# First-half products moved ahead of two phase boundaries, a compact third span of attention, and an earlier fetch of held outputs

## The chip, the cores and the metric

The kernel runs on one core of a Trainium2 chip. The metric is device time in microseconds (us). TensorE (PE in the rows; its weight loads PEld) multiplies, VectorE (DVE), ScalarE (ACT) and GpSimd (POOL) work elementwise, SyncE (SP) issues the DMAs. SBUF is the working memory, PSUM (8 banks of 128 x 512 fp32) takes what TensorE writes.

## The reference

One step of a two-layer decoder trunk over 512 prompt tokens and 8 x 4 sample tokens, 544 in all, with a model width of 1024. Layer 0 is attention, layer 1 a Mamba-2 (SSD) mixer.

```python
for i in range(DEPTH):
    up, us = rmsnorm(hp, norm_pre[i]), rmsnorm(hs, norm_pre[i])
    if i % N_MIXERS == 0:
        yp, bufs_p = attn_prompt(up, attn_w_in[j], attn_w_out[j])
        ...
    else:
        yp, hp_new, cp_new = ssd_mixer(up, ssd_w_in[j], ...)
        ...
    hp = hp + rmsnorm(yp, norm_post[i])
    hs = hs + rmsnorm(ys, norm_post[i])
```

Attention has three spans, each with its own 16 query heads, 4 key heads and 4 value heads of 128:

```python
DILATED_GROUPS = ((128, 1), (512, 4), (2048, 16))
for g, (win, dil) in enumerate(DILATED_GROUPS):
    o, lse = banded_attention(to_strided(qs[g], dil), to_strided(ks[g], dil),
                              to_strided(vs[g], dil), win // dil)
y = merge_groups(outs, lses).reshape(n, l, ATTN_WIDTH).astype(u.dtype)
return (y * jax.nn.silu(gate)) @ w_out, bufs
```

In the third span the 512 prompt tokens fall into 16 residue classes of 32 tokens. A query reads only keys of its own class, so of a block of 128 queries by 128 keys (4 classes) only the four 32 x 32 squares on the diagonal are real; the rest is masked.

## The kernel before

**Phases.** `norm_phase` n0 (L138), `attention_phase` (L622), `mix_phase` m1 (L285), `ssd_phase` (L1549 on), `mix_phase` m2. Each is a block of its own with one instruction stream per engine. Between two blocks all engines meet at a barrier: no instruction of the next block, a DMA's issue included, starts before every engine has ended the last one (in the rows these waits carry lines L2527 to L2543).

**Projections.** The activations are kept feature by feature as `uhi` and `ulo` (high and low part, 8 x 128 features by 544 tokens). A weight tile is 1024 x 128. It is loaded to `w`, ACT copies its high part to `whi`, POOL (attention) or DVE (elsewhere) makes `wlo`, and PE does for each of 8 k blocks three products (whi by uhi, whi by ulo, wlo by uhi) on two halves of 272 tokens: 48 matmuls of 128 x 272 a tile. `w`, `whi`, `wlo` and the output banks have two slots; tile t uses slot t % 2, and may start when its `wlo` is there and the output of tile t-2 has been taken (`proj_free`). Each phase has these output banks as its own (`proj`, in the mix phase `acc`).

**Small items.** Between the quarters of a projection tile PE runs items of a hand-written table (ATTN_AHEAD for the group whose tiles are being made, ATTN_BEHIND for the group before it; SCAN and SETUP with slot times in the SSD phase, where a tile has four slots). Four head groups go through 22 tiles each. Items here: S (scores of a head in a span, L928), SC and SN (scores of the samples, L943), PT (transpose of the scaled probabilities of a unit to `small`, L902, then an ACT copy to `probs_t`, L1060), and, one PT later, `weigh` (L1002), which multiplies them by the values.

**Norm phase n0.** For five blocks of rows: square sum (ACT), inverse and `normed` (DVE, L254), transposes (PE, L191), high (ACT) and low part (DVE, L259). It also splits the first two weight tiles (`w_low` L263).

**Attention, start.** SP issues weight tiles 2 and 3, then the tables cos, sin, masks, mask_s, order and member (L817 to L822). DVE's first instruction waits for all six:

```python
dve.wait_ge(consts_in, 96)
```

Tile 0 is a key tile: DVE rotates it (L1187 to L1190) and then frees its output slot, which tile 2 needs.

**Attention, end.** The last stage does 8 output tiles. Near its end ACT and DVE split the operands of the rest of that product over `uhi` and `ulo` (L1105, L1329), k block by k block as PE's last tile gives them free; four of the eight come back from DRAM first (L834, the held outputs), issued by SP in its step t == 6.

**Mix phase.** PE ends the product, turns rows back, then DVE and ACT norm rows, add the residual (L508), and, in m1, do the pre-norm of layer 1 with PE transposes (L390), `uhi` (L440) and `ulo` (L529) as in n0. The transposes use the banks of `acc`.

**SSD, start.** SP issues the rows of PAR, then the dt weights and three vectors (`wd_in`, L1735), weight tiles 2 and 3, six tables. ACT's first work waits for the dt vectors (L2107). On PE the item PAR stands in slot 1, DT 0 in slot 4 and DT 1 in slot 7.

## Time and profile before

| | us |
|---|---|
| median of three runs | 1431.95 (1427.76 to 1433.5) |
| the profiled execution, its own time | 1431.52 |
| its span in the trace | 1429.7 |
| PE busy / PEld busy | 1336.1 (93%) / 1284.0 (90%) |
| DVE busy / ACT busy / POOL busy | 781.6 / 641.8 / 467.8 |

Stages of the span: n0 up to 24.8, attention to 821.7, m1 to 903.3, SSD to 1363.2, m2 to the end. PE has gaps only around the four boundaries and in parts of the SSD phase. A matmul in the trace may be one record or two: one on plain fp32 data (S, SC, SN, `weigh`) leaves two, one of the projections or a transpose leaves one.

### The profile page before, as it was taken

Reading aid. Unit: us, or ns where it says so; the run is one execution under the profiler, and the core shown is the slowest. Engines: PE = TensorE matmul, PEld = TensorE weight load, DVE = VectorE, ACT = ScalarE, POOL = GpSimd, SP = SyncE. Lnnn points to the kernel's source line nnn. Section 1 sums busy time; section 2 is a strip of 40 time slices with the busy share of each in tenths; the row PEclk is TensorE's granted clock in tenths of the full one; section 3 lists DMA queues with packets and bytes.
Section 4 is the critical chain, followed back from the end, with each engine's and each line's share of the span. In section 5 each row is a group of like instructions: output and inputs, shape, how many; then the busy total and the mean of one; then the engine's idle time right before and its main releaser. Section 6 shows DMA issues by size and latency. Waiting matters only on the chain. (4 is left out here: it accounts for less than half of the span.)

```text
span 1429.7 us, 29707 instructions
## 1 busy us (share of the span) xinstructions
PE 1336.1 (93%) x11026; PEld 1284.0 (90%) x11026; DVE 781.6 (55%) x1493; ACT 641.8 (45%) x1425; POOL 467.8 (33%) x399
## 2 busy tenths in 40 slices
PE   5999999999999999999999896899999988989996
PEld 5999999999899999999999895798888978878996
DVE  4454435454345444355453136577979678686444
ACT  4333433343334334343344334465676655654332
POOL 0555422454324543235522212003334144142011
PEclk9999999999999999999999998899999999999998
DMA  5574333743335633357422252534545626523251
GB/s 183 147 208 120 85 105 98 219 125 99 89 101 159 170 99 92 94 175 226 104 72 77 76 181 88 139 86 126 161 115 156 197 63 199 185 73 105 83 160 70
DMA packets 313415, 182.62 MB, mean 128 GB/s; under 512 B 75232, under 2 KB 302256, under 8 KB 312880
## 3 DMA queue, kind: packets, MB, share of 16 engines
q1 hardware_dynamic: 313264, 180.64, 44.4%
q8 instruction: 91, 1.49, 0.4%
q14 instruction: 60, 0.49, 0.1%
HBM read 155.01 MB, written 46.41 MB: 141 GB/s over the span
## 5 line engine op out<-in xcount | busy, mean ns | idle before, releaser
L1385 POOL TENSOR_TENSOR wlo<-w,whi 128x1024 fp32r<-128x1024 f32 x95 | 228.3, 2403 | 473.6 <-ACT whi L1043 473.6
L892 PE MATMUL at_proj<-uhi,whi 128*128 128x272 f32 x1536 | 334.8, 299 | 7.1 <-PEq L2527 2.5
L892 PE MATMUL at_proj<-uhi,wlo 128*128 128x272 f32 x1536 | 319.3, 289 | 0.0
L892 PE MATMUL at_proj<-ulo,whi 128*128 128x272 f32 x1536 | 318.7, 289 | 0.0
L1043 ACT ACTIVATE whi<-w 128x1024 fp32r<-128x1024 f32 x95 | 100.7, 1060 | 352.8 <-PE at_proj L892 325.5
L892 PEld LDWEIGHTS at_proj<-uhi,whi 128*128 128x128 f32 x1536 | 240.9, 190 | 9.8 <-issue 5.9
L892 PEld LDWEIGHTS at_proj<-ulo,whi 128*128 128x128 f32 x1536 | 243.2, 190 | 0.0
L892 PEld LDWEIGHTS at_proj<-uhi,wlo 128*128 128x128 f32 x1536 | 241.9, 190 | 0.0
L1860 PE MATMUL sd_proj<-uhi,whi 128*128 128x272 f32 x768 | 173.6, 308 | 7.9 <-DVE ulo L2292 3.3
L1860 PE MATMUL sd_proj<-uhi,wlo 128*128 128x272 f32 x768 | 163.6, 295 | 0.0
L1860 PE MATMUL sd_proj<-ulo,whi 128*128 128x272 f32 x768 | 163.4, 295 | 0.0
L1860 PEld LDWEIGHTS sd_proj<-uhi,whi 128*128 128x128 f32 x768 | 126.2, 196 | 18.4 <-issue 7.2
L1187 DVE TENSOR_TENSOR at_straight<-at_proj,at_cos 128x544 f32<-128x544 f32 x60 | 43.4, 724 | 165.9 <-PE at_proj L892 139.5
L1860 PEld LDWEIGHTS sd_proj<-ulo,whi 128*128 128x128 f32 x768 | 125.6, 196 | 0.0
L1860 PEld LDWEIGHTS sd_proj<-uhi,wlo 128*128 128x128 f32 x768 | 125.0, 196 | 0.0
L2259 DVE TENSOR_TENSOR wlo<-w,whi 128x1024 fp32r<-128x1024 f32 x47 | 60.3, 1284 | 50.5 <-ACT whi L2012 50.5
L1053 ACT ACTIVATE at_probs<-at_probs,at_neg_top 128x128 f32<-128x128 f32 (+1 forms) x192 | 79.5, 415 | 2.1 <-ACT yg L1085 0.8
L1060 ACT ACTIVATE at_probs_t<-at_small 128x512 f32<-128x512 f32 x64 | 36.5, 570 | 74.2 <-PE at_small L902 73.8
L1212 DVE TENSOR_TENSOR at_probs<-at_small,at_masks 128x512 f32<-128x512 f32 x32 | 22.1, 691 | 85.1 <-PE at_small L928 84.3
L2269 DVE SCALAR_TENSOR_TENSOR sd_conv<-raw,sd_par,sd_conv 128x568 f32<-128x568 f32 x72 | 64.0, 889 | 0.9
L1002 PE MATMUL at_out_t<-at_probs_t,at_v_rows 128*128 128x128 f32 x480 | 64.2, 277 | 0.0
L355 PE MATMUL m_acc<-uhi,whi 128*128 128x272 f32 x256 | 55.0, 296 | 9.3 <-PEq L2532 6.1
(301 smaller groups left out, 2275.7 us busy)
## 6 DMA issues: line engine op xcount, KB each, us to landing
w<-in_attn_w_in_dram SPq DMA_DIRECT2D x88, 512.0 KB, 4.4
...
```

Source lines behind the costliest of these rows:

```text
L355: last = pe.matmul(acc[:, r, h, 0:HALF], a[:, r, k * P:(k + 1) * P], b[:, k, h * HALF:(h + 1) * HALF], start=(k == 0 and a is whi and b is ...
L892: last = pe.matmul(proj[:, r, h, 0:HALF], a[:, r, kk * P:(kk + 1) * P], b[:, kk, h * HALF:(h + 1) * HALF], start=(kk == 0 and a is whi and ...
L1002: last = pe.matmul(strided(out_t[h % 2][:, :], w_, qt), v_rows[:, w_, kt, :], square(probs_t[:, n % 2, j * P:(j + 1) * P], w_), start=(SLO ...
L1043: act.activation(whi[:, t % PAIR], w[:, t % PAIR], ACT.Copy).then_inc(whi_ready, 1)
L1053: last = act.activation(x, x, ACT.Exp, bias=neg_top[:, w_, qt, h:h + 1], scale=SCALE, accum_out=den[:, w_, qt, h:h + 1])
L1060: act.activation(dst, src, ACT.Copy).then_inc(signal, 1)
L1187: dve.tensor_tensor(two(straight[:, :]), halves(x), two(cos[:, :]), ALU.mult).then_inc(turned_ready, 1)
L1212: last = dve.tensor_tensor(blocks(dst, 4), blocks(b[:, :], 4), masks[:, w_, :].unsqueeze(1).broadcast_to([P, 4, P]), ALU.add)
L1385: pool.tensor_tensor(wlo[:, r], w[:, r], whi[:, r].bitcast(F32), ALU.subtract).then_inc(wlo_ready, 1)
L1860: last = pe.matmul(proj[:, r, h, 0:HALF], a[:, r, kk * P:(kk + 1) * P], b[:, kk, h * HALF:(h + 1) * HALF], start=(kk == 0 and a is whi and ...
L2259: dve.tensor_tensor(wlo[:, r], w[:, r], whi[:, r].bitcast(F32), ALU.subtract).then_inc(wlo_ready, 1)
L2269: dve.scalar_tensor_tensor(out=x, in0=raw[:, n % 2, k:k + COMP], scalar=par[:, e % 2, t, NB * PRE + k:NB * PRE + k + 1], in1=x, op0=ALU.mu ...
```

## The change

1. `proj` becomes one PSUM tile that all phases share (`acc` in the mix phases is the same). The new `first_half` does the 24 matmuls of a tile on tokens 0 to 271. n0 and m1 call it for tiles 0 and 1 of the next phase; attention and SSD then do only the second half of these two tiles. In n0 the transposes get two pairs of banks instead of four; in m1 they move from `acc` to `back`.
2. In m1 the steps of the pre-norm stand in a new order on DVE, ACT and PE.
3. Third span: scores are made as sixteen 32 x 32 products instead of four of 128 x 128, and mask, maximum, exp and scale run on 128 columns instead of 512. PT of this span becomes PW: no PE transpose and no ACT copy; DVE transposes 32 x 32 squares and spreads them with one multiplication to a 128 x 512 tile with zeros between (`widen`), which `weigh` reads.
4. The held outputs are issued at t == 4 instead of t == 6.

```diff
+def first_half(pe, proj, ring, uhi, ulo, r, ks):
+    _, whi, wlo = ring
+    for kk in ks:
+        for a, b in ((whi, uhi), (whi, ulo), (wlo, uhi)):
+            last = pe.matmul(proj[:, r, 0, 0:HALF], a[:, r, kk * P:(kk + 1) * P], b[:, kk, 0:HALF],
+                             start=(kk == 0 and a is whi and b is uhi), stop=(kk == KD - 1 and a is wlo))
+    return last
```

Norm phase, PE:

```diff
+            def turn(i):
...
+            for i in range(TT - 1):
+                turn(i)
+            pe.wait_ge(lo_ready, 3)
+            pe.wait_ge(parted, 1)
+            first_half(pe, proj, ring, uhi, ulo, 0, range(KD // 2))
+            turn(TT - 1)
+            first_half(pe, proj, ring, uhi, ulo, 0, range(KD // 2, KD))
+            pe.wait_ge(parted, PAIR)
+            first_half(pe, proj, ring, uhi, ulo, 1, range(KD)).then_inc(halved, 1)
+            pe.wait_ge(halved, 1)
```

Mix phase, PE and ACT (DVE's steps are reordered likewise, its order is add 0, add 1, inverse 0, norm 0, inverse 1, add 2, norm 1, low 0, inverse 2, norm 2, low 1, add 3, low 2, inverse 3, add 4, norm 3, inverse 4, norm 4, low 3, low 4):

```diff
+                pe.wait_ge(rows_ready, KD)
+                pe.wait_ge(weighted_last, 1)
+                for i in range(3):
+                    turn_back(i)
+                pe.wait_ge(lo_ready, 3)
+                pe.wait_ge(wlo_ready, KD + 1)
+                pe.wait_ge(fm_ready, KD)
+                first_half(pe, acc, ring, uhi, ulo, 0, range(KD // 2))
+                turn_back(3)
+                first_half(pe, acc, ring, uhi, ulo, 0, range(KD // 2, KD))
+                pe.wait_ge(wlo_ready, KD + PAIR)
+                first_half(pe, acc, ring, uhi, ulo, 1, range(KD // 2))
+                turn_back(4)
+                first_half(pe, acc, ring, uhi, ulo, 1, range(KD // 2, KD)).then_inc(halved, 1)
+                pe.wait_ge(halved, 1)
...
+                square_sum(0)
+                row_root(0)
+                square_sum(1)
+                row_root(1)
+                square_sum(2)
+                high(0)
+                row_root(2)
+                high(1)
+                square_sum(3)
+                high(2)
+                row_root(3)
+                square_sum(4)
+                high(3)
+                row_root(4)
+                high(4)
```

Attention:

```diff
-                    if g is None and t == 6:
+                    if g is None and t == 4:
...
+                        for h in range(1 if isinstance(g, int) and g == 0 and t < PAIR else 0, 2):
...
+                        if w_ < 2:
+                            last = pe.matmul(b[:, j * P:(j + 1) * P], q[:, h, qt * P:(qt + 1) * P],
+                                             k[:, kt * P:(kt + 1) * P], start=True, stop=True)
+                            continue
+                        for c in range(4):
+                            at = slice(qt * P + SQ * c, qt * P + SQ * (c + 1))
+                            last = pe.matmul(b[SQ * c:SQ * (c + 1), SQ * j:SQ * (j + 1)], q[:, h, at], k[:, at],
+                                             start=True, stop=True)
...
+                if w_ == 2:
+                    pe.wait_ge(wide_ready, NH * g + h + 1)
+                    x = wide[:, h % 2]
+                else:
+                    pe.wait_ge(probs_t_ready, len(TURNED) * g + TURNED.index(n) + 1)
+                    x = probs_t[:, TURNED.index(n) % 2]
...
+            def widen(g, h):
+                dve.wait_ge(scaled_ready, len(HEADS) * g + HEADS.index(("PW", h, 2, 0)) + 1)
+                dve.transpose(compact_t[:, :], probs[:, h, SLOT[2, 0], 0:P]).then_inc(compact_ready, 1)
+                dve.wait_ge(compact_ready, NH * g + h + 1)
+                dve.wait_ge(head_done, len(HEADS) * g + (HEADS.index(("PW", h - 2, 2, 0)) + 1 if h >= 2 else 0))
+                dve.tensor_tensor(wide[:, h % 2].rearrange("p (i r m) -> p i r m", i=4, r=4),
+                                  blocks(compact_t[:, :], 4).unsqueeze(2).broadcast_to([P, 4, 4, SQ]),
+                                  member[:, 1].unsqueeze(1).unsqueeze(3).broadcast_to([P, 4, 4, SQ]), ALU.mult) \
+                    .then_inc(wide_ready, 1)
```

SSD:

```diff
+                        for h in range(1 if i < PAIR else 0, 2):
```

PE around the last transposes of n0 and the branch into attention, before (`n_turned` takes the transposes, `at_proj` tile 0):

```order
L191 MATMUL n_turned<-ident,n_normed 128x128 x32
L191 MATMUL n_turned<-ident,n_normed 128x32 x8
L145 UNCONDITIONAL_BRANCH
L879 UNCONDITIONAL_BRANCH
L892 MATMUL at_proj<-uhi,whi 128x272 x2
L892 MATMUL at_proj<-ulo,whi 128x272 x2
L892 MATMUL at_proj<-uhi,wlo 128x272 x2
L892 MATMUL at_proj<-uhi,whi 128x272 x2
```

The same place now (`proj` is the shared tile; all rows of `proj` ahead of the branch are `first_half`):

```order
L143 MATMUL proj<-uhi,wlo 128x272
L143 MATMUL proj<-uhi,whi 128x272
L143 MATMUL proj<-ulo,whi 128x272
L143 MATMUL proj<-uhi,wlo 128x272
L203 MATMUL n_turned<-ident,n_normed 128x32 x8
L143 MATMUL proj<-uhi,whi 128x272
L143 MATMUL proj<-ulo,whi 128x272
L143 MATMUL proj<-uhi,wlo 128x272
L143 MATMUL proj<-uhi,whi 128x272
L143 MATMUL proj<-ulo,whi 128x272
L143 MATMUL proj<-uhi,wlo 128x272
L143 MATMUL proj<-uhi,whi 128x272
```

The last transposes (128x32) now stand between `first_half` matmuls: 12 of tile 0 ahead of them, then 12 of tile 0 and 24 of tile 1 up to the branch.

PE at the end of m1 and into SSD, before:

```order
L369 MATMUL m_back<-ident,m_fm 32x128
L390 MATMUL m_acc<-ident,m_normed 128x128 x32
L390 MATMUL m_acc<-ident,m_normed 128x32 x8
L292 UNCONDITIONAL_BRANCH
L1843 UNCONDITIONAL_BRANCH
L1860 MATMUL sd_proj<-uhi,whi 128x272 x2
L1860 MATMUL sd_proj<-ulo,whi 128x272 x2
L1860 MATMUL sd_proj<-uhi,wlo 128x272 x2
L1860 MATMUL sd_proj<-uhi,whi 128x272 x2
```

Now (the same end of the product, then the first three blocks' transposes and tile 0):

```order
L391 MATMUL m_back<-ident,m_fm 32x128
L413 MATMUL m_back<-ident,m_normed 128x128 x24
L143 MATMUL proj<-uhi,whi 128x272
L143 MATMUL proj<-ulo,whi 128x272
L143 MATMUL proj<-uhi,wlo 128x272
L143 MATMUL proj<-uhi,whi 128x272
```

and the first slots of SSD up to the item PAR:

```order
L1972 MATMUL proj<-uhi,whi 128x272
L1972 MATMUL proj<-ulo,whi 128x272
L1972 MATMUL proj<-uhi,wlo 128x272
L1972 MATMUL proj<-uhi,whi 128x272
L1972 MATMUL proj<-ulo,whi 128x272
L1972 MATMUL proj<-uhi,wlo 128x272
L1958 MATMUL sd_small<-ident,sd_par_rows 128x29 x6
L1972 MATMUL proj<-uhi,whi 128x272
L1972 MATMUL proj<-ulo,whi 128x272
L1972 MATMUL proj<-uhi,wlo 128x272
```

Behind the first three blocks' transposes come 12 + 12 + 12 + 12 matmuls of `first_half`, with those of block 3 behind the first twelve and those of block 4 behind the third; PAR now comes after 12 matmuls of SSD instead of 24.

PE in attention, S of the first head in the third span and the quarter around it, before:

```order
L892 MATMUL at_proj<-ulo,whi 128x272 x2
L892 MATMUL at_proj<-uhi,wlo 128x272 x2
L928 MATMUL at_small<-at_k,at_q 128x128 x4
L892 MATMUL at_proj<-uhi,whi 128x272 x2
L892 MATMUL at_proj<-ulo,whi 128x272 x2
```

Now:

```order
L978 MATMUL proj<-ulo,whi 128x272 x2
L978 MATMUL proj<-uhi,wlo 128x272 x2
L1020 MATMUL at_small<-at_k,at_q 32x32 x16
L978 MATMUL proj<-uhi,whi 128x272 x2
L978 MATMUL proj<-ulo,whi 128x272 x2
```

Four matmuls became sixteen, in the same place. SP at the end of the last attention stage, before (`mixed` is the DRAM copy, `at_probs` the place it comes to):

```order
L772 DMA at_v_cache<-in_cache_kv_w_dram 128x4x128 x3
L776 DMA at_v_cache<-in_cache_kv_w_dram 16x4x128 x4
L767 DMA w<-in_attn_w_out_dram 128x8x128 x6
L834 DMA at_probs<-mixed 128x544 x4
L629 UNCONDITIONAL_BRANCH
```

Now:

```order
L858 DMA at_v_cache<-in_cache_kv_w_dram 128x4x128 x3
L862 DMA at_v_cache<-in_cache_kv_w_dram 16x4x128 x4
L853 DMA w<-in_attn_w_out_dram 128x8x128 x5
L920 DMA at_probs<-mixed 128x544 x4
L853 DMA w<-in_attn_w_out_dram 128x8x128
L712 UNCONDITIONAL_BRANCH
```

The four loads moved ahead of the last weight tile.

## Rows read from the trace of the kernel before

**Rows 1.** Stretches: start:end, length; busy us (count) per engine; PEclk, DMA share, GB/s.

```profile
24.80:39.20 14.40, 14.38 (x96) 14.40 (x97) 2.17 (x3) 1.06 (x1) 3.89 (x3) 1.00 0.64 200
39.20:815.60 776.40, 768.26 (x6703) 754.96 (x6701) 342.82 (x678) 296.77 (x711) 313.01 (x212) 1.00 0.46 126
```

**Rows 2.** Instructions in time, n0 into attention: start, duration, engine, [idle before].

```profile
18.81 1.22 DVE L263 TENSOR_TENSOR wlo<-w,whi 128x1024 fp32r<-128x1024 f32 x1
...
24.62 0.99 SPq L767 DMA_DIRECT2D w<-in_attn_w_in_dram  x2
...
34.94 0.72 DVE L1187 TENSOR_TENSOR at_straight<-at_proj,at_cos 128x544 f32<-128x544 f32 x1 [11.13 <-DMA at_member<-in_member_dram]
...
36.45 0.72 DVE L1190 TENSOR_TENSOR at_crossed<-at_proj,at_sin 64x544 f32<-64x544 f32 x1
```

**Rows 3.** The same view, PE: a score item of the third span (x8).

```profile
140.25 0.41 PE L892 MATMUL at_proj<-ulo,whi 128*128 128x272 f32 x2
140.50 0.41 PE L892 MATMUL at_proj<-uhi,wlo 128*128 128x272 f32 x2
140.75 1.05 PE L928 MATMUL at_small<-at_k,at_q 128*128 128x128 f32 x8
...
141.90 0.41 PE L892 MATMUL at_proj<-ulo,whi 128*128 128x272 f32 x2
```

**Rows 4.** The same view, PE: the 32-column score item SN of the samples.

```profile
164.71 0.41 PE L892 MATMUL at_proj<-uhi,wlo 128*128 128x272 f32 x2
165.05 0.40 PE L943 MATMUL at_small<-at_ks,at_qs 128*32 128x32 f32 x24
...
165.73 0.41 PE L892 MATMUL at_proj<-ulo,whi 128*128 128x272 f32 x2
```

**Rows 5.** The same view, PE: a PT of the third span, then `weigh`.

```profile
766.47 0.60 PE L902 MATMUL at_small<-ident,at_probs 128*128 128x128 f32 x4
766.90 1.06 PE L1002 MATMUL at_out_t<-at_probs_t,at_v_rows 128*128 128x128 f32 x8
```

**Rows 6.** The same view: attention into m1, and (last row) SSD into m2.

```profile
801.19 6.39 SPq L767 DMA_DIRECT2D w<-in_attn_w_out_dram  x2
807.69 2.27 SPq L834 DMA_DIRECT2D at_probs<-mixed  x4
...
814.75 2.30 ACT L1105 ACTIVATE uhi<-at_probs 128x544 fp32r<-128x544 f32 x4 [3.50 <-DMA at_probs<-mixed]
...
817.99 2.62 DVE L1329 TENSOR_TENSOR ulo<-yg,uhi 128x544 fp32r<-128x544 f32 x4
...
821.70 0.79 PE L355 MATMUL m_acc<-uhi,whi 128*128 128x272 f32 x2 [6.07 <-PEq L2532]
...
825.02 0.61 PE L355 MATMUL m_acc<-ulo,whi 128*128 128x272 f32 x2
825.47 0.41 PE L355 MATMUL m_acc<-uhi,wlo 128*128 128x272 f32 x2
...
1363.16 0.49 PE L355 MATMUL m_acc<-uhi,whi 128*128 128x272 f32 x2 [3.19 <-PEq L2543]
```

**Rows 7.** The same view, end of m1: transposes, low parts.

```profile
897.62 1.23 DVE L529 TENSOR_TENSOR ulo<-m_acc,uhi 128x1024 fp32r<-128x1024 f32 x1
...
897.72 1.97 PE L390 MATMUL m_acc<-ident,m_normed 128*128 128x128 f32 x8 [1.45 <-DVE m_normed L524]
...
900.78 1.55 DVE L529 TENSOR_TENSOR ulo<-m_acc,uhi 128x1024 fp32r<-128x1024 f32 x2 [0.75 <-ACT uhi L440]
```

**Rows 8.** The same view, start of SSD.

```profile
903.19 0.32 SPq L1722 DMA_DIRECT2D sd_par_rows<-in_state_conv_dram  x1
...
912.97 0.42 ACT L2107 ACTIVATE sd_wdhi<-y 128x256 fp32r<-128x256 f32 x1 [11.41 <-DMA sd_rows<-in_ssd_d_dram]
...
913.98 0.31 PE L1898 MATMUL sd_small<-uhi,sd_wdhi 128*32 128x272 f32 x1 [0.41 <-DVE sd_wdlo L2278]
...
924.47 0.41 PE L1860 MATMUL sd_proj<-uhi,whi 128*128 128x272 f32 x2
```

225 lines of the change are left out of this document (124 added, 101 removed).

## The prediction

> **What bounds the kernel now.** I read the busy times of the engines by stretch first. From 39.2 to 815.6 us, nearly all of attention, PE is busy for 768.3 of 776.4 us [rows 1], while DVE, the next, has 343. So in attention a microsecond of PE work taken away is a microsecond won, as long as no new wait opens. The order in time then shows PE idle at the boundaries between phases. Here the reader must look past PE, at what the first tiles of the new phase wait for: the issue of DMAs begins only behind the barrier [rows 2, 8], and some loads are waited for ten microseconds later. I use four measures throughout. A projection matmul at TensorE's full clock (2.4 GHz) takes 0.1256 us from start to start (0.25 for a pair [rows 3]); at the low clock (1.2 GHz) 0.227 us (0.45 for a pair [rows 6]). From the end of the last work to the first DMA behind a barrier it takes 0.86 us (low part ends at 902.33 [rows 7], SP at 903.19 [rows 8]). And after 6.07 us without a matmul the clock is low for the first 16 to 17 matmuls (821.70 to 825.47), after 3.19 us it is not: the first pair at 1363.16 lasts 0.49 us, against 0.79 us at 821.70 [rows 6]. A restart at the low clock costs 16 x 0.101 = 1.6 us.
>
> **Part A, norm phase into attention.** 48 matmuls leave the attention phase, 48 x 0.1256 = 6.0 us; the 14.4 us from 24.8 to 39.2 hold the 96 matmuls of tiles 0 and 1 [rows 1], 12.1 at the full clock and 2.3 of low clock. What do they cost ahead of the boundary? `first_half` waits for the low part of block 2 and for `w_low` of tile 0, whose subtraction ends at 18.81 + 1.22 = 20.03 [rows 2]. PE was mostly idle before, so I take the low clock: 12 matmuls to 22.8, the small transposes (about 1 us, half of what the large take in [rows 7]) to 23.8, 12 more at either clock to 25.3 or 26.5, 24 at the full clock to 28.3 or 29.5, and 0.2 for the last to end. The first DMA of attention then starts at 29.4 to 30.5 instead of 24.62; I take 29.6, that is 5.0 later. Here the gain is lost: DVE's first instruction waited for the tables until 34.94, 10.3 us after SP's start, and its rotation lasts to 36.45 + 0.72 = 37.2 [rows 2]. Before, that hid behind tiles 0 and 1, with 2.0 us to spare before tile 2 at 39.2. Now tiles 0 and 1 are 6.0 us of second halves, and tile 2 waits for the output slot of tile 0, so for the same tables: 29.6 + 10.3 + 2.2 = 42.1, plus 0.1. That is 3.0 us later than before, and as PE has then been idle for over 6 us, 1.6 to 2.3 us of low clock come on top. A = +4.8, bounds +3.5 (clock up early, no slow restart) and +6.5.
>
> **Part B, the compact third span.** There are 4 groups x 4 heads = 16 score items and 16 PTs of this span. Score item: from the pair at 140.50 to the pair at 141.90 it is 1.40 us; less two pairs (0.50) the item takes 0.90 us [rows 3]. Its sixteen 32 x 32 products leave 32 records. The nearest row is SN: 12 products of 32 columns by 32, 24 records, in turn on the four quarters of the output rows as here. From 164.71 to 165.73 it is 1.02, less 0.50: 0.52 us, 0.32 of it the records themselves (165.05 to 165.37, as its length allows [rows 4]), 13 ns each. So 32 records take 0.52 + 8 x 0.013 = 0.63, or 0.69 if all of it scales; I take 0.65. Gain 0.25 x 16 = 4.0 us, bounds 3.4 and 4.3.
> The Trainium skill speaks against this edit (TensorE: Matmul & The Clock Gate, section "Wait — 56ns, not 53.3ns?"): from start to start a matmul never takes less than about 25 ns, however few its columns. By that rule 32 records take 0.80 us, the gain is 0.1 x 16 = 1.6, and the whole sum comes out 2.4 us higher; the trace's 24 records in 0.32 us do not agree, unless one counts the 12 products they come from.
> PT: 766.47 to 766.90, 0.43 us [rows 5], goes, 16 x 0.43 = 6.9 us. What replaces it is on DVE: a transpose and a 128 x 512 multiplication, against three passes that shrink from 512 to 128 columns. DVE is idle for more than half of the stretch [rows 1], and the probabilities are scaled five items ahead of their use, so I cost it at nothing; were that cover gone, an item would wait up to the 0.7 us of one such pass, 16 times. The `weigh` ahead of a PW loses the 0.43 us of transposes that hid part of its ACT copy; it has the `weigh` before it left (0.8 us) and I allow 0.1 us in a few places, inside the bounds. B = -10.9, bounds -13 (PE's small waits shrink too) and -7.
>
> **Part C, held outputs.** SP issued them at 807.69, right behind a weight tile (the two tiles' issues run from 801.19 to 807.58); ACT waited 3.50 us for their landing and began the split at 814.75, 7.06 after the issue; DVE ended it at 817.99 + 2.62 = 820.61, and m1 began at 821.70 [rows 6]. Two steps earlier means behind the weight tile issued at 801.19: issued about 801.6, landed 808.7, before PE's last tile gives its first k block free (its 48 matmuls end at 821.70 - 6.07 = 815.63 [rows 6], so they began at 809.6 and the first eighth ends at 810.4). Then ACT and DVE follow PE block by block and only the last block is left behind PE: ACT 0.6, DVE 0.7, barrier, which puts m1 at 818.2. The same end of the SSD phase, which is not held up by a fetch, has a gap of 3.19 us [rows 6], which gives 818.8. I take 818.6: -3.1 us, and with a gap of 3.0 us the clock stays up, -1.6. C = -4.7, bounds -3.0 and -5.2. The four DMAs now stand ahead of one weight load; that waits for its slot until 807.2 anyway.
>
> **Part D, m1 into SSD.** In the new order of DVE and ACT the low part of block 2 still comes at about 898.5: it ended at 897.62 + 1.23 = 898.85 before [rows 7], and the steps ahead of it are fewer, but ACT squares block 3 between two high parts. So `first_half` can't fill the idle time before that. From 898.5: 12 matmuls at the low clock to 901.2, transposes of block 3 (1.8 of the 1.97 us [rows 7]) to 903.0. Continuous work brings the clock up about here: 24 matmuls to 906.0, the last transposes (their rows are normed at 905.9 by my count, since the root of block 4 stands behind high part 3 on ACT) to 907.0, 12 matmuls to 908.5, end 908.7. Before, all engines were done at 902.33. The 6.0 us of work that moved moved the boundary by 6.3 us: SP at 909.5 instead of 903.19. And again there is a load behind it: the dt weights allow ACT to start 9.8 us after SP and DT 0 to start 10.8 us after it, 913.98, where PE was just 0.41 us early [rows 8]. Now PE has 12 + 18 matmuls and PAR before DT 0, some 4.5 us, and waits: DT 0 at 909.5 + 10.8 = 920.3. From DT 0 to tile 2 there are 24 + 18 + 24 matmuls, 8.3 us, plus 0 to 1.8 of low clock: 929.2, against 924.47 [rows 8]. D = +4.7, bounds +3.5 and +7. No later stage gives this back, since all of SSD hangs on the same start.
>
> **Sum**, against the profiled execution's own 1431.52 us, which is 0.4 under the median: +4.8 - 10.9 - 4.7 + 4.7 = -6.1, so **1425.4 us**. With all four at their low ends it would be 1420.3, with all at their high ends 1435.
>
> **Rivals.**
> R1, the two boundaries pay: the tables and dt vectors arrive early enough. Then tile 2 starts 6.3 us behind SP at 35.9, A = -3.3; in SSD 96 matmuls and PAR, 12.6 us, lead to 922.1, D = -2.4; the sum is -21.3: 1410.2 us. For it: some of that delay could be queueing behind other traffic. Against it: DVE's idle of 11.13 us and ACT's of 11.41 us both end at a DMA that is issued behind the barrier [rows 2, 8], and the edit leaves the issues where they are. 7 in 100.
> R2, slower: the 32 x 32 products do not overlap. Their weights come from two tensors that change with every product, where SN keeps one operand for four. If a record then takes as long as one of the full-size item, 0.90 / 8 = 0.11 us [rows 3], an item costs 3.5 us and the kernel 45 us more: 1471. It ends above 0.5% slower once an item takes over 1.48 us, 46 ns a record. Against it the 13 ns of [rows 4]. 6 in 100.
> R3, the wide tile comes late: PW waits one DVE pass each, or other engines fall behind a faster PE, 16 x 0.5 = +8: 1433.5. Against it DVE's idle share and the five items' lead. 6 in 100.
> R4, issuing bounds the small products: a record takes what one of SN's products of two records took, 0.32 / 12 = 27 ns [rows 4]. An item is then 0.86 us, the gain on scores 0.6 instead of 4.0: 1428.8. 5 in 100. The page named in part B would have it so.
>
> **How the numbers follow.** The forecast has 76 in 100. A measurement of this kernel tells 0.5%, about 7 us, from no change: faster means under 1424.8. The forecast lies 0.6 us above that, so its chance parts nearly in half: 0.33 faster, 0.42 same, 0.01 slower. R1 adds 0.07 to faster, R4 0.05 to same, R3 0.04 to same and 0.02 to slower, R2 0.06 to slower. Together 0.40, 0.51, 0.09. The range leaves R1 and R2 out, goes 1.8 us below the low ends towards R1, and drops the last 2.5 us of the high ends: 1418.5 to 1432.5.
>
> **What would show it.** A: the first DMA of attention near 29.6, DVE's first instruction still some 10.3 us behind it and ended by the tables, PE idle for about 6 us before tile 2 near 42. B: per item 0.65 us of records at 32 x 32, no transposes of the third span, PE as dense as before. C: the fetch issued one weight tile earlier, the split paced by PE, a gap near 3 us at full clock. D: `first_half` starting near 898.5, SP near 909.5 (shifted by A to C), a PE wait before DT 0. The prediction is wrong if tile 2 starts with no wait in either phase (R1), or if an item of the third span takes longer than before (R2).

## The result, and the profile after

The changed kernel takes **1440.33 us** (median of 19 runs, 1432.56 to 1448.19), the kernel before 1432.53 (median of 19, 1427.76 to 1437.26): a ratio of 1.0059, 95% interval 1.0042 to 1.0076. In a second set of runs (after_again, below) it was 1.0024, 0.9995 to 1.0053, just not clear of 1. I had forecast 1425.4. The profiled execution took 1437.81 us, 1436.0 of it span.

The instructions of the profile after, in time: start, duration, engine, line, [idle before <- releaser]. First the norm phase into attention, answering [rows 2].

```profile
20.11 0.56 PE L143 MATMUL proj<-uhi,whi 128*128 128x272 f32 x1 [1.02 <-DVE wlo L286]
...
31.56 1.00 SPq L853 DMA_DIRECT2D w<-in_attn_w_in_dram  x2
...
42.78 0.72 DVE L1286 TENSOR_TENSOR at_straight<-proj,at_cos 128x544 f32<-128x544 f32 x1 [17.75 <-DMA at_member<-in_member_dram]
...
45.21 0.79 PE L978 MATMUL proj<-uhi,whi 128*128 128x272 f32 x2 [7.21 <-DVEq L1292]
```

As forecast, the tables are waited for behind the later start of SP, and now nothing hides them: PE is idle for 7.21 us. SP began at 31.56 instead of 29.6, and the third tile (the one that I call tile 2) at 45.2 instead of 42.1; before it was 39.29.

A score item of the third span, answering [rows 3]:

```profile
147.84 0.41 PE L978 MATMUL proj<-uhi,wlo 128*128 128x272 f32 x2
148.18 0.46 PE L1020 MATMUL at_small<-at_k,at_q 128*32 128x32 f32 x32
...
148.92 0.41 PE L978 MATMUL proj<-ulo,whi 128*128 128x272 f32 x2
```

From the pair at 147.84 to that at 148.92 it is 1.08, less 0.50: 0.58 us against 0.90. The item is even shorter than the 0.65 of the forecast. The end of the held outputs' step and the start of the state-space phase, answering [rows 6] and [rows 8]:

```profile
815.54 3.58 DVE L1442 TENSOR_TENSOR ulo<-at_probs,uhi 128x544 fp32r<-128x544 f32 x4 [15.29 <-ACT uhi L1204]
819.04 2.62 DVE L1442 TENSOR_TENSOR ulo<-yg,uhi 128x544 fp32r<-128x544 f32 x4
...
822.78 0.57 PE L377 MATMUL proj<-uhi,whi 128*128 128x272 f32 x2 [3.73 <-PEq L2644]
823.15 0.65 PE L377 MATMUL proj<-ulo,whi 128*128 128x272 f32 x2
...
915.10 0.63 PE L1958 MATMUL sd_small<-ident,sd_par_rows 29*128 29x29 f32 x5 [2.35 <-DMA sd_par_rows<-in_ssd_conv_b_dram]
...
921.31 0.31 PE L2010 MATMUL sd_small<-uhi,sd_wdhi 128*32 128x272 f32 x1 [1.77 <-DVE sd_wdlo L2390]
...
929.59 0.41 PE L1972 MATMUL proj<-uhi,whi 128*128 128x272 f32 x2
```

The gap ahead of m1 shrank from 6.07 to 3.73 us (3.0 forecast). The fetch is no longer waited for, but the split isn't paced by PE either: VectorE makes its eight low parts without a gap from 815.54 to 821.66, and PE's last product ends at 819.05, so four of them, 2.6 us, come behind PE, where the forecast left one. The products behind the gap run at the low clock all the same: the pair of 0.65 us. In the state-space phase PE waits for the parameters' DMA (2.35 us, not forecast) and for the dt weights (1.77 us).

So the items did what they should, and still attention from the third tile to its last matmul shrank only from 776.3 to 773.8 us. The next view says why. It cuts the same traces into stretches (start:end, length; busy us per engine; PEclk, DMA share, GB/s); these are all the stretches inside attention in which PEclk is low, of the kernel after and then of the kernel before:

```profile
41.00:49.00 8.00, 3.79 (x19) 3.82 (x20) 2.17 (x3) 0.00 (x0) 3.81 (x3) 0.57 0.32 77
191.00:199.00 8.00, 8.00 (x41) 8.00 (x42) 4.44 (x12) 0.03 (x1) 1.52 (x1) 0.57 0.69 179
362.00:366.00 4.00, 4.00 (x22) 4.00 (x22) 1.45 (x6) 0.55 (x1) 0.00 (x0) 0.57 0.18 54
379.00:387.00 8.00, 6.15 (x30) 6.15 (x31) 3.48 (x9) 0.00 (x0) 0.00 (x0) 0.57 0.69 187
550.00:554.00 4.00, 4.00 (x22) 3.96 (x22) 1.45 (x6) 1.05 (x2) 0.00 (x0) 0.58 0.04 12
761.00:765.00 4.00, 4.00 (x44) 3.15 (x43) 1.94 (x1) 0.28 (x1) 1.39 (x1) 0.57 0.34 102
```

```profile
371.00:375.00 4.00, 2.94 (x13) 2.95 (x14) 3.01 (x8) 0.00 (x0) 0.00 (x0) 0.57 0.86 244
545.00:549.00 4.00, 4.00 (x22) 3.95 (x22) 1.27 (x6) 1.78 (x4) 0.83 (x1) 0.57 0.00 0
```

Length times (1 - PEclk) is the clock lost in such a spell: 8 x 0.43 = 3.4 us or 4 x 0.43 = 1.7 us. After the restart at 41 to 49 there are five, 11.9 us; before there are two, 3.4. Attention at the full clock did shrink by some 11 to 13 us, and 8.5 of it went into the clock. The lists of all runs give the same for the whole kernel. I call span x (1 - mean granted clock) the **lost clock** and span x clock the **rest**. (The lost clock counts low spells in which PE is idle too, so it is no pure loss of time.) The profile before has 1429.7 x 0.030 = 43 and 1387, the 88 runs of the kernel before in the four sets below 44.1 and 1389.0; the changed kernel's 19 runs have 52.4 and 1386.3 in the mean. All of the slowdown stands in the first number. And it isn't idle time at a low clock: of the stretches with low PEclk, 72 us in the profile after and 89 us in that of after_again have PE busy, against 55 and 60 us in the two profiles of before, while the idle part is 31 to 33 us in all four. Which parts bring it, only parts run alone can tell.

### The profile page after: what moved, and what is told of

It is laid out like the page before. It is cut to its first block and busy times, and to the rows that moved or that the text cites. A ratio compares the mean times of both kernels' runs of the same rounds, so it can differ in the third digit from the quotient of the medians.

```text
span 1436.0 us, 30380 instructions
## 1 busy us (share of the span) xinstructions
PE 1335.1 (93%) x11346; PEld 1277.4 (89%) x11346; DVE 787.2 (55%) x1525; ACT 627.7 (44%) x1409; POOL 466.2 (32%) x399
## 3 DMA queue, kind: packets, MB, share of 16 engines
q1 hardware_dynamic: 313264, 180.64, 44.1%
## 5 line engine op out<-in xcount | busy, mean ns | idle before, releaser
L978 PE MATMUL proj<-uhi,whi 128*128 128x272 f32 x1520 | 335.4, 301 | 11.5 <-DVEq L1292 7.2
L978 PE MATMUL proj<-uhi,wlo 128*128 128x272 f32 x1520 | 319.1, 291 | 0.0
L978 PE MATMUL proj<-ulo,whi 128*128 128x272 f32 x1520 | 318.6, 290 | 0.0
L978 PEld LDWEIGHTS proj<-uhi,whi 128*128 128x128 f32 x1520 | 240.8, 192 | 14.9 <-issue 11.1
L978 PEld LDWEIGHTS proj<-ulo,whi 128*128 128x128 f32 x1520 | 243.2, 191 | 0.0
L978 PEld LDWEIGHTS proj<-uhi,wlo 128*128 128x128 f32 x1520 | 241.5, 192 | 0.0
L1972 PE MATMUL proj<-uhi,whi 128*128 128x272 f32 x752 | 169.6, 306 | 7.4 <-DVE ulo L2404 3.7
L1972 PE MATMUL proj<-uhi,wlo 128*128 128x272 f32 x752 | 160.3, 293 | 0.0
L1972 PE MATMUL proj<-ulo,whi 128*128 128x272 f32 x752 | 159.7, 293 | 0.0
L1972 PEld LDWEIGHTS proj<-uhi,whi 128*128 128x128 f32 x752 | 122.4, 194 | 17.6 <-issue 6.9
L1286 DVE TENSOR_TENSOR at_straight<-proj,at_cos 128x544 f32<-128x544 f32 x60 | 43.4, 724 | 169.1 <-PE proj L978 141.7
L1972 PEld LDWEIGHTS proj<-ulo,whi 128*128 128x128 f32 x752 | 121.7, 193 | 0.0
L1972 PEld LDWEIGHTS proj<-uhi,wlo 128*128 128x128 f32 x752 | 121.5, 194 | 0.0
L1152 ACT ACTIVATE at_probs<-at_probs,at_neg_top 128x256 f32<-128x256 f32 (+2 forms) x192 | 74.3, 388 | 2.1 <-ACT yg L1184 0.8
L624 POOL TENSOR_TENSOR m_rows<-m_rows,m_w_post 128x512 f32<-128x512 f32 x14 | 17.9, 1280 | 138.8 <-ACT m_squared L449 138.8
L1530 POOL TENSOR_TENSOR at_q<-at_straight,at_crossed 128x512 f32<-128x512 f32 x48 | 62.7, 1307 | 0.0
L377 PE MATMUL proj<-uhi,whi 128*128 128x272 f32 x256 | 55.9, 300 | 6.9 <-PEq L2644 3.7
```

The lines of the kernel that those rows point to most:

```text
L377: last = pe.matmul(acc[:, r, h, 0:HALF], a[:, r, k * P:(k + 1) * P], b[:, k, h * HALF:(h + 1) * HALF], start=(k == 0 and a is whi and b is ...
L624: pool.tensor_tensor(x, x, w_post[:, at].unsqueeze(1).broadcast_to([P, TT - 1, P]), ALU.mult)
L978: last = pe.matmul(proj[:, r, h, 0:HALF], a[:, r, kk * P:(kk + 1) * P], b[:, kk, h * HALF:(h + 1) * HALF], start=(kk == 0 and a is whi and ...
L1152: last = act.activation(x, x, ACT.Exp, bias=neg_top[:, w_, qt, h:h + 1], scale=SCALE, accum_out=den[:, w_, qt, h:h + 1])
L1286: dve.tensor_tensor(two(straight[:, :]), halves(x), two(cos[:, :]), ALU.mult).then_inc(turned_ready, 1)
L1530: pool.tensor_tensor(dst, a, b, ALU.add).then_inc(qk_ready, 1)
```

## Experiments

The kernels ran in four sets, each on a chip of its own together with the kernel before (its own rows below). Medians are of all runs, the last two columns means over them.

| kernel | runs | median us | ratio (95%) | lost clock | rest |
|---|---|---|---|---|---|
| before (set 1) | 12 | 1434.4 | | 43.7 | 1389.6 |
| compact_only | 5 | 1427.4 | 0.9931 (0.9904 to 0.9959) | 45.3 | 1378.5 |
| compact_and_fetch | 5 | 1423.4 | 0.9912 (0.9886 to 0.9939) | 42.6 | 1377.8 |
| norm_half_only | 8 | 1442.8 | 1.0052 (1.0034 to 1.0070) | 46.6 | 1393.9 |
| mix_half_only | 5 | 1443.0 | 1.0061 (1.0037 to 1.0085) | 48.7 | 1392.6 |
| before (set 2) | 21 | 1434.4 | | 44.0 | 1389.3 |
| stats_ahead | 5 | 1420.3 | 0.9893 (0.9871 to 0.9915) | 42.0 | 1376.3 |
| norm_tables_first | 11 | 1435.8 | 1.0011 (0.9988 to 1.0034) | 43.1 | 1392.2 |
| mix_par_early | 11 | 1436.1 | 1.0010 (0.9997 to 1.0022) | 42.7 | 1392.2 |
| before_again | 1 | 1435.5 | | 45.9 | 1387.8 |
| before (set 3) | 28 | 1434.7 | | 44.5 | 1388.9 |
| stats_ahead_only | 11 | 1431.3 | 0.9983 (0.9962 to 1.0004) | 43.0 | 1387.3 |
| halves_only | 6 | 1448.4 | 1.0089 (1.0061 to 1.0118) | 48.7 | 1397.6 |
| after_again | 11 | 1440.2 | 1.0024 (0.9995 to 1.0053) | 51.9 | 1385.8 |
| all_repaired | 11 | 1428.6 | 0.9958 (0.9934 to 0.9982) | 44.5 | 1382.5 |
| before (set 4) | 27 | 1433.6 | | 43.9 | 1388.4 |
| wait_filled | 11 | 1440.5 | 1.0043 (1.0025 to 1.0060) | 45.5 | 1393.2 |
| fed_clock | 11 | 1438.2 | 1.0024 (1.0006 to 1.0042) | 48.2 | 1387.6 |
| ssd_filled | 11 | 1440.7 | 1.0034 (1.0011 to 1.0057) | 42.8 | 1395.0 |
| tail_filled | 4 | 1417.4 | 0.9877 (0.9850 to 0.9903) | 33.3 | 1382.7 |

### The parts alone

The kernels of set 1 are the kernel before with the diff's hunks of one or two parts: compact_only has PW, `widen` and the 32x32 products, and compact_and_fetch has the sooner fetch beside them:

```diff
-                    if g is None and t == 6:
+                    if g is None and t == 4:
```

norm_half_only and mix_half_only have `first_half` in one phase and the halved first tiles behind it.

> The kernel before with the compact third span alone (32x32 score products, the PW item, DVE's transpose and widening; no first halves, held outputs fetched at t == 6 as before). Before stands at 1432.5 us. Theory: the items themselves got shorter as forecast (-10.9), but the clock falls more often in attention: the profile of the changed kernel has five falls there where before has two, some 8 us more of lost clock, and they come from the compact span. Then this kernel gives 1430 to 1434 us, with span x (1 - granted clock) at 47 us or more (42.9 in the profile of before). Rival: the falls come from where the first half has shifted the work (the 6 us by which attention starts later) or are chance; then this kernel shows the whole gain, 1421 to 1424 us, with the lost clock near 43 us.

> The kernel before with the compact third span and the held outputs fetched at t == 4, without the first halves. Theory: 2.3 us less than the kernel with the compact span alone, for the gap that shrank from 6.07 to 3.73 us in front of the first mixing product: 1427.5 to 1431.5 us if the clock eats the compact span's gain, 1418.5 to 1421.5 us if it doesn't. Rival: the fetch moves other waits, and nothing is gained (equal to the compact span alone within 1 us).

> The kernel before with only the first halves of the first two tiles' products done in the norm phase. Theory: the third tile begins 6.1 us later, as in the profile of the changed kernel (45.2 against 39.2), and restarts at the low clock, another 1.6 to 2.5 us: 1440 to 1441 us. Rival (the prediction's term): +3.5 to +5, 1436 to 1437.5 us. Second rival (the later start moves clock falls): over 1442 us, with more falls inside attention than the two of before.

> The kernel before with only the first halves done in the first mix phase, for the state-space phase behind it. Theory: +4.2, as the turn-to-third-tile stretch of the changed kernel (52.3 against 48.1 us): 1436 to 1437.5 us. Rival (the last phase's low clock at its start belongs to it too): +6.5, 1439 us. Second rival: the part's cost is taken back by the shorter first tiles: 1432 to 1433 us.

The ranges above start from 1432.5 us, while the kernel before took 1434.4 beside these runs; so I read the ratios, applied to 1432.5. The compact span gave 0.9931, -9.9 us (-13.8 to -5.9). Its 1427.4 lies between my 1430 to 1434 and the rival's 1421 to 1424; by the ratio it is 1422.6, the rival's. Nearly the whole gain is there, and the lost clock of 45.3 (43.7 before) is below the 47 of my theory: if the clock takes a part, these runs don't resolve it. With the fetch it is 1423.4, by the ratio 1419.9, the range for a gain that the clock doesn't eat; the gap ahead of m1 is 3.71 us against 6.29, and the clock is low behind both. The norm phase's half costs 1.0052 (+7.4 us, +4.9 to +10): its 1442.8 is above my 1440 to 1441 (by the ratio 1439.9, at their lower edge), and the second rival's "more falls" is not in its profile, which has two inside attention, as before. The mix phase's half costs 1.0061 (+8.7, +5.3 to +12.2), above all its ranges. Both are more than the prediction had. The third tile of mix_half_only began 54.2 us after the last turn of m1, 48.1 before, so 6.1 us stand at that place. A further 2.8 us of its profile come behind it; the last phase starts at the low clock, as the first rival has it, and as the next profile of the kernel before does too.

> The kernel before with the first halves in both phases, without the compact span and with the held outputs fetched at t == 6. Theory: +7.3 and +8.0 add up, 1448 to 1452 us (span x granted clock some +7 above the 1389.5 of before, lost clock some +8 above its 44). Rival: only one of the two late starts can cost in full, since the falls that the first brings are passed on or taken back before the second: 1443 to 1446 us.

> The changed kernel, unchanged, on one chip with the three below; the kernel before stood at 1434.4 us in the runs so far. Theory: the four parts add up. In the runs' means the compact span gave -9.5, the sooner fetch -3.4, the norm phase's half +7.3, the mix phase's half +8.0, together +2.4; in their medians -7.0, -4.0, +8.4 and +8.5, together +5.9: 1437 to 1441 us. Rival: the parts meet (TensorE comes to the waits of the compact span at another phase when attention starts late, and the clock falls more): +8 or more, 1443 us and above, with span x (1 - granted clock) at 52 us again, where the sum of the parts gives 50.7.

Halves alone: +13.7 us by the medians, against +17 for the two apart; the whole: +5.5 here, +7.8 in the first measurement, against +5.9 for the sum of set 1's medians. By the ratios it is +12.7 against +16.1, and +3.4 and +8.4 against +3.5. Within their intervals the parts add up. No meeting of parts has to be explained, and the lost clock was again 52, where the parts' differences, added to before's, give 50.5.

> The kernel before, unchanged, for a second profile. Theory: where the clock falls is partly chance: the last phase, which began at the full clock in the profile of before and at the low one in the changed kernel (2.5 us of it), may begin at either here, and the attention phase shows two to four falls of 3.4 us where the first profile had two; span x (1 - granted clock) between 42 and 47 us. Rival: the falls belong to the kernel: the same list of falls as in the first profile, and the full clock in the last phase's start.

A second profile of the very same kernel. The start of its last phase, which the first profile passed at the full clock [rows 6]:

```profile
1364.59 0.79 PE L355 MATMUL m_acc<-uhi,whi 128*128 128x272 f32 x2 [3.19 <-PEq L2543]
1365.18 0.66 PE L355 MATMUL m_acc<-ulo,whi 128*128 128x272 f32 x2
```

It began at the low clock this time, behind the same idle time of 3.19 us, and attention held four spells, 8.5 us, where the first profile had 3.4. So where the clock falls differs from one execution to the next of one kernel, and a row such as the 1363.16 of [rows 6] is one throw, not a rule. All 18 profiles of this study have this gap, 3.18 to 3.20 us long; 11 of them begin the last phase at the low clock.

### What the compact span meets: the cached keys

VectorE and TensorE of compact_only around the item M (16 products on `at_parted`, the row statistics of the spans, which VectorE makes with two products of its own), in time:

```profile
345.01 0.15 DVE L1261 TENSOR_SCALAR at_stat_s<-at_stat_s 128x1 f32<-128x1 f32 x1
347.30 2.22 DVE L1382 STREAM_TRANSPOSE at_keys_t<-at_k_cache 128x448 f32<-128x448 f32 x4 [2.14 <-DMA at_k_cache<-in_cache_kv_w_dram]
349.45 0.45 DVE L1289 TENSOR_TENSOR at_parted<-at_stat,at_member 128x128 f32<-128x128 f32 x2
...
349.95 2.29 PE L959 MATMUL at_small<-at_parted,at_order 128*128 128x32 f32 x13 [1.58 <-DVE at_parted L1289]
```

TensorE reaches M's place earlier in the group than before, but the keys of the samples' cache come at SyncE's pace. VectorE waits 2.14 us for them, the two products for M stand behind the transposes, and PE waits 1.58 us behind VectorE; the clock falls from 350 to 358. A second such wait, 1.74 us, comes one group later; the kernel before has one of 1.26. It is not the compact span's alone: norm_half_only, at full width, has two as well, of 0.97 and 1.61 us. Does that order cost something?

```diff
+                            if item == ("KT", 1, 0):
+                                part_stats(g)
                             dve.wait_ge(k_cache_in[s], 16 * KEY_LOADS * (g + 1))
...
-                            part_stats(g)
                             gather(st, g)
```

> The kernel compact_and_fetch (1423.4 us) with one step of VectorE moved: the two products that make at_parted, for which TensorE's item M waits, stand ahead of the four transposes of the second set of cached keys instead of behind them. In both kernels with the compact span VectorE waits 2.1 us there for the DMA of at_k_cache, and TensorE behind it 1.5 to 1.6 us, twice. Theory: the compact span is worth less than forecast since TensorE now comes to that item before the cached keys are in; with the step moved both waits go (-3.1) and with them the clock falls next to them (up to -3.4 each): 1416 to 1420.5 us. Rival: the waits only move behind TensorE's next need of the same keys (the item SC 1), and nothing is gained: 1422.5 to 1424.5 us.

```profile
347.47 0.49 DVE L1289 TENSOR_TENSOR at_parted<-at_stat,at_member 128x128 f32<-128x128 f32 x2 [3.27 <-ACT at_probs L1071]
347.88 2.22 DVE L1384 STREAM_TRANSPOSE at_keys_t<-at_k_cache 128x448 f32<-128x448 f32 x4
...
348.02 1.19 PE L959 MATMUL at_small<-at_parted,at_order 128*128 128x32 f32 x9 [0.60 <-DVE at_parted L1289]
```

The wait fell from 1.5 to 0.60 us; it is now for ScalarE's exponentials. The time fell by 3.1 us, within the theory's range at its upper end, but the two kernels ran in different sets and their intervals overlap (in the means 2.2 us, uncertain by 3.0), so the gain in time is not shown. The spells inside attention point the same way: the four profiles with the compact span and the old order (compact_only, compact_and_fetch, the two of after, without the restart at 40) have 10.2, 8.5, 11.9 and 15.4 us of them, the three with the step moved (stats_ahead, all_repaired, tail_filled) 6.8, 6.8 and 8.5, and eleven without the compact span 1.7 to 8.5, 5.1 in the mean.

There is a second wait that the compact span lengthens, which none of these kernels mends. Ahead of a projection tile of the second group PE stands idle, in before and then in compact_only:

```profile
372.06 0.82 PE L892 MATMUL at_proj<-uhi,whi 128*128 128x272 f32 x2 [2.08 <-issue]
```

```profile
372.14 0.82 PE L897 MATMUL at_proj<-uhi,whi 128*128 128x272 f32 x2 [3.20 <-issue]
```

The seven profiles with the compact span have 2.78 to 3.20 us there, ten of the eleven without it 1.86 to 2.47 (the last, wait_filled, 3.31), and the granted clock falls in this wait or within 1 us of it in all 18. What ends this wait the profile doesn't show.

> The kernel before with only VectorE's two products for item M ahead of the cached keys' four transposes. Theory: the wait for at_parted is there in before in part (one of 1.26 us in the first profile, one of 1.59 us in the second, two of 1.54 us each with the compact span): the gain is about half of the 2.2 us in the runs' means that it gave behind the compact span, 1432.5 to 1434 us. Rival: with the full-width span the wait is covered in most runs, and nothing is gained: within 0.5 us of before. Second rival: it is worth as much as with the compact span, or more: under 1432 us.

1431.3, 3.4 us less by the medians, but 0.9983 with an interval that touches 1. That is the second rival's range; the ratio's (2.4 us) is between it and the theory's. The wait was there before in part, and how much the compact span added to its price stays open.

### What the halves meet: loads behind the barrier

```diff
+            sp.dma_start(cos[:, :], tables["cos"]).then_inc(turns_in, 16)
+            sp.dma_start(sin[:, :], tables["sin"]).then_inc(turns_in, 16)
             for t in range(PAIR):
                 load_w(0, PAIR + t, t)
...
-            dve.wait_ge(consts_in, 96)
+            dve.wait_ge(turns_in, 32)
```

> The kernel norm_half_only (1442.8 us) with the two rotation tables as SyncE's first loads of attention, and VectorE waiting for these two alone ahead of its first rotation. Theory: the cost of the first half in the norm phase is nearly all this wait (7.7 us of idle TensorE ahead of the third tile, and the restart at the low clock behind it); with the tables at SyncE + 7 instead of + 11.2 the third tile begins at 39 to 40 us instead of 43.8, and the low spell there shrinks: 1435 to 1438.5 us. Rival: the cost sits elsewhere (what the later start moves in the rest of attention and behind it): 1440 us or more.

SyncE's first load and TensorE's third tile in norm_half_only, then in norm_tables_first:

```profile
29.71 0.99 SPq L789 DMA_DIRECT2D w<-in_attn_w_in_dram  x2
...
43.84 0.79 PE L914 MATMUL proj<-uhi,whi 128*128 128x272 f32 x2 [7.69 <-DVEq L1215]
```

```profile
31.77 0.35 SPq L838 DMA_DIRECT2D at_cos<-in_cos_dram  x1
...
42.28 0.82 PE L915 MATMUL proj<-uhi,whi 128*128 128x272 f32 x2 [4.07 <-POOL wlo L1410]
```

From SyncE's start the third tile is 10.5 us away instead of 14.1: 3.6 us won, a little less than the theory has (3.8 to 4.8); the tile itself came at 42.28, since SyncE began 2.1 us later. Then the next load is late: PE waits for the low part of the weight tile, which now stands behind the tables. In time it was 7.0 us by the medians (5.9 by the ratios), more than those 3.6: the lost clock fell by 3.5 with it. SyncE's start itself differs by 2 us between profiles (29.71, 31.77, 31.56 in the kernel after). In the two late ones the first 28 and 27 products of the first half last about 0.43 us each, in norm_half_only 12.

The same for the second boundary; `early` holds the first group's nine parameter loads, issued in m1 behind its last weight tile:

```diff
+            for e_dst, e_src in (early or ()):
+                sp.dma_start(e_dst, e_src).then_inc(early_in, 16)
             for i in range(TT):
                 sp.wait_ge(h_ready, i + 1)
...
-            load_par(0)
```

> The kernel mix_half_only (1443.0 us) with the nine loads of the first group's parameters (par_rows) issued in the mix phase instead of at the head of SyncE's queue in the state-space phase. Theory: the cost of the first half there is that the state-space phase's loads start 6.3 us later, and TensorE has too little left to cover them: the wait ahead of item PAR (2.3 us) goes and the wait ahead of item DT 0 (2.1 us) shrinks, since SyncE reaches its weights 3 us sooner; the third tile begins 2.5 to 4 us earlier: 1438 to 1440.5 us. Rival: another load (the skip weights' broadcast, waited for last by ScalarE) sets the item's start wherever it stands, and the gain is under 1.5 us: 1441.5 us or more.

The PE wait ahead of PAR is gone, the one ahead of DT 0 is 2.89 us, and the third tile begins 51.2 us after m1's last turn instead of 54.2. The time fell by 6.9 us, below the theory's range, to 1.0010 of before: nearly the whole cost of the part hung on nine small loads, again more than the 3.0 us at the place, and again the rest of it is lost clock (48.7 to 42.7).

> The changed kernel with the three repairs: VectorE's two products for item M ahead of the cached keys' transposes, the rotation tables as SyncE's first loads of attention with a wait of their own, and the parameters' nine loads of the state-space phase issued in the mix phase. Theory (parts add up in the runs' means): stats_ahead -15.2, norm_tables_first +1.8, mix_par_early +1.5 against before: 1421 to 1425 us, some 16 us under the changed kernel as it is and no better than stats_ahead alone. Rival: the parts meet, and the repairs give less together: 1428 us or more.

1428.6: by the ratios 9.5 us better than after_again, not 16. The theory's sum fails here, and the rival's 1428 stands. In its profile the third tile began at 43.17 behind a wait of 4.85 for the weight tile and again at the low clock. What each repair is worth beside the others stays open; that the halves still cost something beside the repaired compact span (1420.3) doesn't.

### The clock: filling the waits

Three kernels put products of no use, never read, where TensorE waits. In wait_filled:

```diff
+                if isinstance(g, int) and g == 0 and t == PAIR and q == 0:
+                    for _ in range(56):
+                        pe.matmul(out_t[0][:, 0:HALF], uhi[:, 0, 0:P], uhi[:, 0, 0:HALF], start=True, stop=True)
```

> The kernel norm_half_only (1442.8 us median; lost clock, that is span x (1 - granted clock), 46.6 in the runs' mean, rest 1393.9) with 56 products of no use, 128x128 by 272 columns, put on TensorE in the wait for the tables ahead of the third tile (56 x 0.125 = 7.0 of the 7.7 us). Nothing else differs; what they write is never read. Theory: the clock falls there because TensorE stands idle; filled, the low spell of 40 to 47 us in that profile goes, and with it 1.6 to 2.5 us of the part's cost: 1439.5 to 1441.5 us, lost clock 43 to 44.5. Rival: the lost clock comes with the later start as such and turns up elsewhere: 1442 us or more, lost clock 46 or more.

> The kernel mix_half_only (1443.0 us; lost clock 48.7 in the runs' mean) with 12 products of no use ahead of item PAR (a wait of 2.3 us) and 10 ahead of item DT 0 (2.1 us) in the state-space phase. Theory: the low spells at 914 and 921 us of that profile, 1.7 us each, come from TensorE idle in these waits; filled, they go: 1439.5 to 1441.5 us, lost clock 45 to 46. Rival: the clock there is decided by what came earlier (the mixing phase's tail at the low level), and the filling, itself slow at the low clock, delays what is behind it: 1443 us or more.

The wait for the tables and the 3.2 us behind it, in norm_half_only and then in wait_filled; then the two spells of mix_half_only, and the same place in ssd_filled:

```profile
36.20:43.80 7.60, 0.00 (x0) 0.00 (x0) 2.17 (x3) 1.69 (x4) 1.27 (x2) 0.77 0.70 218
43.80:47.00 3.20, 3.16 (x14) 3.19 (x15) 0.00 (x0) 0.00 (x0) 3.20 (x3) 0.50 0.00 0
```

```profile
36.20:43.80 7.60, 7.37 (x59) 7.15 (x58) 1.96 (x3) 1.69 (x4) 1.63 (x1) 1.00 0.76 235
43.80:47.00 3.20, 2.79 (x22) 2.82 (x23) 0.20 (x1) 0.00 (x0) 2.92 (x3) 1.00 0.02 5
```

```profile
914.00:919.00 5.00, 4.35 (x24) 4.21 (x24) 0.00 (x0) 0.00 (x0) 0.00 (x0) 0.66 0.30 50
921.00:926.00 5.00, 4.76 (x26) 3.80 (x27) 2.29 (x4) 3.73 (x9) 0.47 (x3) 0.66 0.90 237
```

```profile
909.00:922.00 13.00, 9.99 (x81) 9.19 (x80) 2.84 (x5) 3.28 (x8) 0.47 (x3) 1.00 0.45 111
```

Filled, the same places run at the full clock. For the wait ahead of the third tile that says that an idle TensorE, not the late start, made the clock fall: the seven other profiles with the half in the norm phase all have a low spell there, begun between 38.9 and 42.4. For the state-space phase one profile is thin evidence, since all_repaired, unfilled and with a wait of 2.70 us, has no low spell there either. Lost clock went from 46.6 to 45.5, not down to the theory's 43 to 44.5, and from 48.7 to 42.8. The times fell to 1.0043 and 1.0034, which agrees with the theories' ranges (1439.5 to 1441.5), but their intervals overlap those of the unfilled kernels: the price in time, 1 to 4 us by the ratios, is not resolved.

> The kernel norm_half_only with 19 products of no use on TensorE in the norm phase's own gaps (10 ahead of the first turn, 3, 3 and 1 ahead of the next ones, 2 ahead of the first half), so that the clock is up when the first half begins at 20.2 us. There its first 12 to 28 products last 0.43 us each, a pitch of 0.23 against 0.125 later. Theory: the first half ends 1.3 to 3 us sooner, SyncE reaches attention's loads that much sooner, and the time falls by as much: 1440 to 1441.5 us. Rival: the filling doesn't lift the clock, or delays the turns behind it: 1442.5 us or more.

1438.2, 1.0024: 4 us less by the ratios, but not by the mechanism named. SyncE began at 29.71 as in norm_half_only, the first pair of attention at 29.91 as there, and there was a low spell at 18 to 22 instead (it is in this kernel's 48.2 of lost clock; for the others the granted clock of this phase is missing, as the last section says). The third tile came at 42.25 instead of 43.84, since the tables did. I leave this one open.

> The kernel stats_ahead (1420.3 us median, 42.0 lost clock) with 27 products of no use on TensorE in the tail of the first mixing phase: 16 ahead of the first turn (the gap of 9.8 us), 1, 6, 3 and 1 ahead of the others. Theory: the clock, low there from 867 to 895 us, is up when the state-space phase begins, its first 12 pairs of products take 0.25 us each instead of 0.45 (-2.4), and the turns 1.0 instead of 2.0 us each where they are waited for: 1415.5 to 1418.5 us, lost clock down by far more than the time (5 to 10), since most of it fell on an idle TensorE. Rival: the clock falls again in the gaps left, or the filling stands in the way of a turn: within 1 us of stats_ahead, or over.

PEclk of stats_ahead and then of tail_filled: m1's tail in two stretches, then the start of the state-space phase.

```profile
866.00:874.00 8.00, 1.00 (x5) 1.00 (x6) 7.57 (x13) 3.85 (x9) 0.92 (x1) 0.58 0.49 198
874.00:889.00 15.00, 7.93 (x37) 6.20 (x35) 11.94 (x17) 6.81 (x12) 0.00 (x0) 0.50 0.12 44
889.00:895.00 6.00, 5.71 (x26) 5.57 (x27) 2.22 (x3) 0.00 (x0) 0.00 (x0) 0.53 0.22 40
```

```profile
866.00:874.00 8.00, 3.82 (x33) 3.63 (x34) 7.57 (x13) 4.63 (x15) 1.86 (x2) 1.00 0.42 169
874.00:889.00 15.00, 8.77 (x62) 7.79 (x62) 12.87 (x17) 6.82 (x12) 0.00 (x0) 0.85 0.17 60
889.00:895.00 6.00, 5.48 (x24) 5.40 (x24) 2.22 (x3) 0.00 (x0) 0.00 (x0) 0.52 0.22 40
```

The filling keeps the clock up through most of the tail, 9 us of lost clock less, and it falls just where the products begin that were to profit. 1417.4 us is the lowest time of the study, but the intervals of 0.9877 and 0.9893 overlap, so the runs don't tell the two apart. Either beats both kernels, by 1.1 to 1.2% of before.

## Why the prediction was wrong

| part | forecast | alone, from the ratio | its rest | its lost clock |
|---|---|---|---|---|
| A, norm half | +4.8 | +7.4 | +4.3 | +2.9 |
| B, compact span | -10.9 | -9.9 | -11.1 | +1.6 |
| C, sooner fetch | -4.7 | -2.7 | -0.7 | -2.7 |
| D, mix half | +4.7 | +8.7 | +3.0 | +5.0 |
| sum | -6.1 | +3.5 | -4.5 | +6.8 |

(Columns 4 and 5: differences from before (set 1), C from compact_only. By the spread of the runs each is uncertain by 1.2 to 2.9 us, so they can't be read term by term: C's gain would be all clock by them, while in the profiles its gap shrank by 2.6 us.)

Most of the waits were the right ones. What failed first is the clock, which I had priced only as restarts at known places: +1.8 in A, -1.6 in C, +0.6 in D, together +0.8. Beside the kernel before (set 3) the changed kernel has 7.4 us more of lost clock. The other terms of the sum come to -6.9, and its rest fell by 3.1 us only: the terms named below were too small in A and D and too large in C.

- **A.** Right: the barrier moves, the tables hold the third tile, and the restart behind the wait is slow. In norm_half_only the first half itself went as forecast: 12 matmuls at the low rate, SP at 29.71 (29.6). Mis-sized is the step "29.6 + 10.3 + 2.2 = 42.1": VectorE could begin 11.7 us behind SP, not 10.3, and the third tile came at 43.84, 4.6 us later than before instead of 3.0. Why the tables landed later stays open. Of the low spell around it only 3.2 us meet a busy TensorE, 1.6 us, as in the sum. In the profile after a second step fails, 12 matmuls at the low clock and "12 more at either clock", then the full one: 27 ran at the low rate, and SP began 2.0 us later than the 29.6 I took. The upper bound of +6.5 was too low for the +7.4 of the ratio, though its interval (4.9 to 10) includes it.
- **B.** Right in size: item 0.58 us, transposes gone. R2 and R4 are out: in the profile after its records take 0.39 us (148.18 to the next pair at 148.57), 12 ns each. A floor of some 25 ns, as the Trainium skill has it (TensorE: Matmul & The Clock Gate, section "Wait — 56ns, not 53.3ns?"), does not hold for a record; it would fit the sixteen products, 24 ns each. R3 is out as it was written, no product waits for the wide tile; but its second half, other engines falling behind a faster PE, came true in small: 3.3 us of waits for `at_parted` in compact_only against 1.3 before, and 1.1 us more ahead of the tile at 372. I had cost this at nothing; the measured -9.9 doesn't tell it from zero.
- **C.** Right: the fetch lands in time. The step that failed is "ACT and DVE follow PE block by block and only the last block is left behind PE: ACT 0.6, DVE 0.7": VectorE's eight low parts take 6.1 us without a gap and end 2.6 us behind PE, so the gap is 3.7 us instead of 3.0. And "with a gap of 3.0 us the clock stays up, -1.6" is false; it rested on the single row 1363.16 of [rows 6], which both before_again and the profile after contradict at the same 3.19 us of idle time.
- **D.** Right: in mix_half_only the first half is at 898.65 (898.5), SP 6.8 us later counted from m1's last turn (6.3), DT 0 held by its load 10.8 us behind SP, as forecast. Not forecast is the wait ahead of PAR; DT 0 hides its 2.3 us, but the clock falls in it too. Third tile +4.2 in the profile after, +6.1 in mix_half_only and +5.9 in after_again: of the step "8.3 us, plus 0 to 1.8 of low clock" the low clock took 0, 1.5 and 1.7 us, where the sum had 0.6. So this place explains up to 1.4 us of the miss; where the rest of the ratio's +8.7 lies stays open, beside the low clock at the start of the last phase.
- **R1**, the boundaries pay, is refuted by both waits; with the loads moved each half alone costs about nothing (1.0010, 1.0011), and still they don't pay; beside the repaired compact span the two cost 9 us (0.9958 against 0.9893).
- The **range** added bounds of durations, but none for how the falls of the clock differ between executions. In the kernel before alone, the runs of the four sets have lost clocks from 37 to 56 us. That, and the two halves, is what lay outside. No lucky error helped: A, C and D all erred to the same side.
